# Two of the 4 MB expert loads of a mixture-of-experts layer issued as 112, 8 and 8 partitions

## The chip, the core and the metric

One core of a Trainium2 chip runs the whole program. The metric is the device time of one execution in microseconds. Two facts of the profile's notation: a DMA is issued by an engine's queue (SPq is that of SyncE), and its packets are moved by the core's 16 DMA engines.

## What is computed

One layer of a decoder trunk on 256 tokens of width 2048, in float32: four mixers side by side, an output projection, a cross attention into 256 memory tokens, and a mixture of experts. Only the last part matters here:

```python
x = x + hier_moe(rms_norm(x, ln_moe_g[l]), moe_w_group[l], moe_b_group[l],
                 moe_w_expert[l], moe_b_expert[l], moe_w_gate[l], moe_w_up[l], moe_w_down[l])

def hier_moe(...):
    ...
    g_idx = jnp.argmax(g_logits, axis=-1)                       # 1 of 4 groups
    top_val, top_idx = lax.top_k(e_logits, EXPERT_TOPK)         # 2 of its 8 experts
    ...
def expert_block(args):
    xblk, e = args
    hid = jax.nn.silu(xblk @ w_gate[e]) * (xblk @ w_up[e])
    return hid @ w_down[e]
```

There are 32 experts. Each has three weights of 4 MB (gate and up are 2048 x 512, down is 512 x 2048), 12 MB together, so that the experts' weights are 384 MB. A token uses two experts.

## The kernel before

The program is written engine by engine; all waits are explicit. The first 550 us hold the mixers, the attention and the router. Then the experts follow, every one of the 32 in order, each on a block of up to 32 tokens (`SLOTS`); experts whose tokens overflow a block get further blocks in a loop with a count read at run time.

For one block PE gathers the chosen tokens (`gather`, L1200) and turns them (`turn_rows`, L1226), multiplies them with the gate and up weights (`gate_up`, L1241, 64 matmuls), turns the result (`turn_hidden`, L1262), multiplies with the down weight (`down`, L1276, 32 matmuls) and adds the weighted rows to their tokens (`combine`, L1289, with DVE's `add`, L2573).

The weights come through five buffers of 4 MB, the "doubles", three in the tile `ring` and two in `late_ring`. One 4 MB load fills one double: partition p takes one contiguous row of 32 KB. SP issues the loads (`whole`, L512), strictly in the order gate, up, down, expert by expert. Before each it waits for the semaphore `pieces_done`, by which PE tells that the double's former weight is used up; a load is thus issued about four loads ahead of its use. On landing, a load adds 16 to the semaphore of its double, one for each of the 16 DMA engines. PE waits for that count in `gate_up` and `down`, by `arrived_main`.

The experts fall into three parts. Experts 0 to 8 use the semaphores `head_in`; the loop follows, in which expert 9 is also loaded; experts 10 to 31 use `main_in`. `main_load(n)` issues the n-th load of this last part: expert 10 + n // 3, weight n % 3. There are 66, of which the last expert's three are cut into smaller transfers, further below in the same block. `arrived_main` computes how many loads have gone to a double up to expert j, times 16:

```python
uses = len([n for n in range(3 * j) if MAIN_DOUBLES[n % 5] == d])
return main_in[d], 16 * uses
```

The tile names of the profile are these: `ring` and `late_ring` for the doubles, `x_gathered` for the turned tokens, `gate_up`, `hidden`, `y_slots` and `tokens_out` for the results of the steps above.

Of the kernel before, what the change touches and what calls it, by code (L numbers as in the profile page):

```python
# [31 lines left out]
KD = D // P  # L32
GW = 512
GC = GW // P
# [18 lines left out]
MAIN = FIRST + 1  # L53
# [123 lines left out]
LOOP_DOUBLES = [DOUBLES[(HEAD_LOADS - 3 + q) % 5] for q in range(3)]  # L177
MAIN_DOUBLES = [DOUBLES[(HEAD_LOADS + k) % 5] for k in range(5)]
MAIN_LOADS = 3 * (N_EXP - MAIN - 1)


def freed(n, first):

    return PPE * (first + n // 3) + (PPE if n % 3 == 2 else 4)


def places_of(doubles):

    g, u, d = doubles
    return [2 * g, 2 * u, 2 * g + 1, 2 * u + 1, 2 * d, 2 * d + 1]  # L190
# [38 lines left out]
def trunk(nc, inp, const_d, bucket_d, out):  # L229
    ctx = ExitStack()  # L230
    with ctx:
# [6 lines left out]
        main_in = [ctx.enter_context(nc.semaphore(f"main_in{i}")) for i in range(MOE_RING // 2)]  # L238
# [218 lines left out]
        def whole_source(e, q):  # L457

            w = inp[("moe_w_gate", "moe_w_up", "moe_w_down")[q]][0]
            return w.rearrange("e (p k) n -> p e k n", p=P)[:, e, :, :]  # L460
# [9 lines left out]
        def moe_double(d):  # L470

            w = ring if d < RING // 4 else late
            a = (d if d < RING // 4 else d - RING // 4) * 2 * WIDE
            return w[:, a:a + 2 * WIDE]
# [17 lines left out]
        def _(sp):  # L492
# [18 lines left out]
            def whole(e, q, d, arrived):  # L511
                sp.dma_start(moe_double(d).rearrange("p (k n) -> p k n", k=KD if q < 2 else GC),  # L512
                             whole_source(e, q)).then_inc(arrived[d], 16)
# [3 lines left out]
            for i, key in enumerate(PIECES):  # L517
                if i >= FRONT_RING:

                    g, q = PIECES[i - FRONT_RING]  # L520
# [66 lines left out]
            for h in range(2):  # L587
# [4 lines left out]
                for k in (4 * h, 8 + 4 * h):  # L592
                    a = FF * k
# [11 lines left out]
                whole(STREAM + n // 3, n % 3, DOUBLES[n % 5], head_in)  # L605

            def main_load(n):
                whole(MAIN + 1 + n // 3, n % 3, MAIN_DOUBLES[n % 5], main_in)

            sp.wait_ge(head["pieces_done"], freed(HEAD_LOADS - 5, STREAM))  # L610
            main_load(0)
            sp.wait_ge(s["tables"], 1)
            n_reg = sp.value_load(n_blk[0:1, 0:1], min_val=2, max_val=TABLE)
            with sp.Fori(1, n_reg) as i:
                e = sp.value_load(blk_e[0:1, bass.ds(i, 1)], min_val=0, max_val=N_EXP - 1)
                for q in range(3):
                    sp.wait_ge(head["pieces_done"], tally(i, PPE, 4 if q < 2 else PPE))
                    d = LOOP_DOUBLES[q]
                    sp.dma_start(moe_double(d).rearrange("p (e k n) -> p e k n", e=1, k=KD if q < 2 else GC),
                                 whole_source(bass.ds(e, 1), q)).then_inc(head_in[d], 16)  # L620
            main_load(1)
            for n in range(2, MAIN_LOADS - 3):
                sp.wait_ge(main["pieces_done"], freed(n - 2, 0) if n < 5 else freed(n - 5, 1))
                main_load(n)

            sp.wait_ge(main["pieces_done"], freed(MAIN_LOADS - 7, 1))
            g, u, d = (MAIN_DOUBLES[(MAIN_LOADS - 3 + q) % 5] for q in range(3))
            for q, a in ((0, g), (1, u)):
                sp.dma_start(moe_slot(2 * a).rearrange("p (k n) -> p k n", k=8),
                             whole_source(N_EXP - 1, q)[:, 0:8, :]).then_inc(main_in[a], 16)  # L630
            for q, a in ((0, g), (1, u)):
                for h in range(2):
                    k = 8 + 4 * h
                    sp.dma_start(moe_slot(2 * a + 1)[:, PIECE * h:PIECE * h + PIECE].rearrange("p (k n) -> p k n", k=4),
                                 whole_source(N_EXP - 1, q)[:, k:k + 4, :]).then_inc(s["tail_high" if h else "tail_low"], 16)
            sp.wait_ge(main["pieces_done"], freed(MAIN_LOADS - 6, 1))
            w = whole_source(N_EXP - 1, 2)
# [39 lines left out]
        def _(pe):  # L677
            task = [0]

            def fill(name, cols=512, parts=P):  # L680

                assert TASKS[task[0]] == name, (name, TASKS[task[0]])
                if task[0] >= 8:
                    pe.wait_ge(s["psum_drained"], task[0] - 7)
                task[0] += 1
                return bank[(task[0] - 1) % 8][0:parts, 0:cols]
# [99 lines left out]
            b = fill("params", cols=TAPS + NROW)  # L786
# [182 lines left out]
            b = fill("wq0")  # L969
# [209 lines left out]
            b = fill("pos0", cols=32)  # L1179
# [32 lines left out]
            b = fill("pos1", cols=32)  # L1212
# [4 lines left out]
            b = fill("cnt", cols=32)  # L1217
# [50 lines left out]
            def down(f, b, arrived_at, slots):  # L1268

                pe.wait_ge(f["hid"], tally(b, 1, 1))  # L1270
                for k in range(4):
                    if k % 2 == 0:
                        pe.wait_ge(*arrived_at(slots[k // 2]))
                    w = moe_slot(slots[k // 2])[:, PIECE * (k % 2):PIECE * (k % 2) + PIECE]
                    for c in range(COLS):
                        mm = pe.matmul(rows_bank[SLOTS * c:SLOTS * c + SLOTS, :], hidden_chunk(k),  # L1276
                                       w[:, 512 * c:512 * c + 512], start=k == 0, stop=k == 3)
                    if k % 2:
                        mm.then_inc(f["pieces_done"], 1)
# [12 lines left out]
            def last_half():  # L1292

                pe.wait_ge(main["hid"], N_EXP - MAIN)
                pe.wait_ge(*arrived_main(place[4]))
                w = moe_slot(place[4]).rearrange("p (k n) -> p k n", k=4)
                for k in range(4):
                    for c in range(COLS):
                        mm = pe.matmul(last_rows[0][SLOTS * c:SLOTS * c + SLOTS, 0:256], hidden_chunk(k),
                                       w[:, k, 256 * c:256 * c + 256], start=k == 0, stop=k == 3)  # L1300
                mm.then_inc(s["last_down"], 1)
# [136 lines left out]
            for j in range(last + 1):  # L1438
                place = places_of(LOOP_DOUBLES if j == 0 else [MAIN_DOUBLES[(3 * (j - 1) + q) % 5] for q in range(3)])

                def arrived_main(slot, j=j):
                    d = slot // 2
                    if j == 0:
                        return head_in[d], n_reg * 16 + 16 * (HEAD_LOADED[d] - 1)
                    uses = len([n for n in range(3 * j) if MAIN_DOUBLES[n % 5] == d])
                    return main_in[d], 16 * uses

                straight(main, j, last, place, arrived_main)
                if j < last:
                    down(main, j, arrived_main, place[4:6])  # L1450
# [1214 lines left out]
```

## Time and profile before

| | us |
|---|---|
| median of 3 runs | 1445.69 |
| lowest, highest | 1441.6, 1445.75 |
| the profiled execution | 1444.81 |
| its span, first to last instruction | 1442.9 |
| PE busy (matmul) | 1223.2 |
| DVE busy | 607.9 |
| ACT busy | 217.2 |

The granted TensorE clock was 0.918 of full speed over the span. Core-wide, 478.83 MB were moved by DMA, 332 GB/s over the span. Busy times of different engines overlap, and so do not add up to the span. How to read the time: the profiled execution is one run, and its span leaves out 1.9 us before the first and after the last instruction.

### The profile page before, as it was taken

The numbers are of one execution on the slowest core, as the hardware profiler recorded it, in microseconds if no ns is written. First come the engines' busy times: TensorE is split into PE (matmuls) and PEld (weight loads), VectorE is DVE, ScalarE is ACT, GpSimd is POOL, SyncE is SP. The second block draws the span as 40 slices with busy tenths as digits, with TensorE's granted clock in tenths as the row PEclk, the third lists the DMA queues.
The fourth block names the chain that finished last, engine by engine and source line by source line (L and its number), as shares of the span: only waits on it lengthen the run. The fifth ranks groups of instructions, "written<-read, shape, count | busy, mean of one in ns | idle before, by whom it ended". The sixth has DMA issues, their size and how long they took to land.

```text
span 1442.9 us, 16078 instructions
## 1 busy us (share of the span) xinstructions
PE 1223.2 (85%) x6717; PEld 580.2 (40%) x6717; DVE 607.9 (42%) x1281; ACT 217.2 (15%) x460; POOL 15.3 (1%) x31
## 2 busy tenths in 40 slices
PE   6999999999999999987677877877777778777877
PEld 5884564565885543232222222222222223222222
DVE  4889999678553452323122231223122222122122
ACT  4202011373011411101000100000000000000001
POOL 4000000000000000000000000000000000000000
PEclk9999999999999999999778988888898978889888
DMA  9433452522547579999999999999999999999997
GB/s 296 153 146 124 154 204 110 201 84 88 175 176 270 212 290 426 423 434 431 429 431 426 430 434 426 431 435 429 429 434 431 427 433 432 429 433 429 431 425 275
DMA packets 62392, 478.83 MB, mean 332 GB/s; under 512 B 13493, under 2 KB 21045, under 8 KB 44784
## 3 DMA queue, kind: packets, MB, share of 16 engines
q1 hardware_dynamic: 61056, 477.44, 80.2%
q8 instruction: 54, 0.88, 0.3%
q0 software_dynamic: 864, 0.25, 0.1%
q10 hardware_dynamic: 400, 0.10, 0.0%
q14 instruction: 18, 0.15, 0.0%
HBM read 475.67 MB, written 2.11 MB: 331 GB/s over the span
## 4 chain that ended last, share of the span: by engine, by line
PE 57%; DMA 32%; DVE 5%; ACT 4%; issue 1%; SPq 0%; DVEq 0%; ACTq 0%
DMA ring<-in_moe_w_up_dram 19%; PE bank L1241 12%; PE bank L715 10%; DMA late_ring<-in_moe_w_up_dram 8%; PE bank L1276 7%; PE bank L736 5%; PE bank L1006 5%; PE bank L1200 3%; PE bank L1262 3%; DMA late_ring<-in_moe_w_down_dram 2%; PE bank L1126 2%; DMA ring<-in_w_in_dram 2%; PE bank L1289 2%; PE bank L997 2%; PE bank L1082 1%
## 5 line engine op out<-in xcount | busy, mean ns | idle before, releaser
L1241 PE MATMUL bank<-ring,x_gathered 128*32 128x512 f32 x1216 | 263.1, 689 | 55.9 <-DMA late_ring<-in_moe_w_up_dram 32.6
L1241 PE MATMUL bank<-late_ring,x_gathered 128*32 128x512 f32 x832 | 210.8, 683 | 36.9 <-DMA ring<-in_moe_w_up_dram 35.6
L2573 DVE TENSOR_TENSOR tokens_out<-tokens_out,bank 128x512 f32<-128x512 f32 x240 | 148.6, 681 | 192.8 <-PE bank L1289 192.8
L2563 DVE SCALAR_TENSOR_TENSOR hidden<-hidden,bank 128x128 f32<-128x128 f32 x32 | 9.2, 288 | 359.6 <-ACT hidden L1794 359.6
L715 PE MATMUL bank<-ring,hT 128*128 128x512 f32 (+2 forms) x416 | 156.3, 536 | 3.4 <-ACT hT L1483 2.6
L1241 PEld LDWEIGHTS bank<-ring,x_gathered 128*32 128x32 f32 x1216 | 68.7, 124 | 151.9 <-issue 149.0
L1200 PE MATMUL bank<-x_tok,select 128*32 128x512 f32 x512 | 115.9, 1032 | 7.3 <-DVE select L2472 4.2
L715 PEld LDWEIGHTS bank<-ring,hT 128*128 128x128 f32 x416 | 78.6, 190 | 78.5 <-issue 67.0
L1276 PE MATMUL bank<-ring,hidden 128*32 128x512 f32 x560 | 90.9, 808 | 18.2 <-DVE hidden L2565 18.2
L1241 PEld LDWEIGHTS bank<-late_ring,x_gathered 128*32 128x32 f32 x832 | 55.0, 123 | 111.7 <-issue 107.3
L1289 PE MATMUL bank<-y_slots,weight_slots 32*128 32x512 f32 x496 | 72.3, 653 | 32.1 <-ACT y_slots L1799 21.7
L1262 PE MATMUL bank<-consts,gate_up 128*128 128x64 f32 x256 | 65.9, 401 | 25.0 <-ACT gate_up L1792 25.0
L736 PE MATMUL bank<-hT,ring 128*128 128x256 f32 x384 | 83.9, 380 | 2.4 <-issue 1.4
L1262 PEld LDWEIGHTS bank<-consts,gate_up 128*128 128x128 f32 x256 | 62.1, 327 | 51.8 <-issue 51.0
L736 PEld LDWEIGHTS bank<-hT,ring 128*128 128x128 f32 x384 | 72.6, 190 | 13.0 <-ACT hT L1541 1.5
L1276 PE MATMUL bank<-late_ring,hidden 128*32 128x512 f32 x416 | 64.1, 773 | 13.6 <-DVE hidden L2565 12.3
L1792 ACT ACTIVATE gate_up<-bank 128x512 f32<-128x512 f32 x32 | 19.1, 597 | 341.3 <-PE bank L1241 341.3
L2528 DVE TENSOR_TENSOR x_gathered<-bank,gain_cols 128x512 f32<-128x512 f32 x32 | 22.1, 692 | 100.8 <-PE bank L1226 100.8
L1289 PEld LDWEIGHTS bank<-y_slots,weight_slots 32*128 32x128 f32 x496 | 19.5, 183 | 110.0 <-DVE tokens_out L2573 59.4
L1276 PEld LDWEIGHTS bank<-ring,hidden 128*32 128x32 f32 x560 | 21.0, 141 | 72.8 <-issue 52.0
L2097 DVE SCALAR_TENSOR_TENSOR knT<-z_padded,param_cols,knT 128x256 f32<-128x256 f32 x120 | 47.6, 484 | 0.0
L1799 ACT ACTIVATE y_slots<-bank 128x512 f32<-128x512 f32 x31 | 18.5, 597 | 180.9 <-PE bank L1276 180.9
(438 smaller groups left out, 1182.0 us busy)
## 6 DMA issues: line engine op xcount, KB each, us to landing
ring<-in_moe_w_up_dram SPq DMA_DIRECT2D x19, 4096.0 KB, 39.2
ring<-in_moe_w_down_dram SPq DMA_DIRECT2D x16, 4096.0 KB, 29.8
ring<-in_moe_w_gate_dram SPq DMA_DIRECT2D x16, 4096.0 KB, 38.4
late_ring<-in_moe_w_down_dram SPq DMA_DIRECT2D x13, 4096.0 KB, 29.1
late_ring<-in_moe_w_gate_dram SPq DMA_DIRECT2D x12, 4096.0 KB, 39.6
late_ring<-in_moe_w_up_dram SPq DMA_DIRECT2D x10, 4096.0 KB, 39.3
ring<-in_w_in_dram SPq DMA_DIRECT2D x20, 1024.0 KB, 9.1
ring<-in_w_out_dram SPq DMA_DIRECT2D x16, 1024.0 KB, 5.7
```

The lines of the kernel that those rows point to most:

```text
L715: mm = pe.matmul(b, lhs(i)[:, P * tt:P * tt + P], piece_view(key)[:, c, at:at + cols], start=i == 0, stop=i == n - 1)
L736: mm = pe.matmul(b[:, T * f:T * f + T], piece_view(key)[:, c, a:a + P], rhs(i), start=i == 0, stop=i == n - 1)
L997: mm = pe.matmul(b, OT[:, 4 * q + c, P * tt:P * tt + P], piece_view((f"wo{n}", q))[:, c, :], start=i == (1 if tt == 0 else 0) and c == 0, ...
L1006: mm = pe.matmul(b, rows(j), weights(j), start=j == 0, stop=j == 7)
L1126: mm = pe.matmul(b, XOT[:, k, P * n:P * n + P], piece_view(("co", c))[:, k, :], start=k == 0, stop=k == XA_H - 1)
L1200: mm = pe.matmul(rows_bank[SLOTS * c:SLOTS * c + SLOTS, :], SEL[:, tt, :], X[:, tt, :].rearrange("p (f k) -> p k f", k=KD)[:, 4 * c:4 * c ...
L1241: mm = pe.matmul(gu_bank[SLOTS * c:SLOTS * c + SLOTS, :], XGT[:, at, n % 4, n // 4, :], pieces[c % 2][:, FF * (n % 8):FF * (n % 8) + FF], ...
L1262: mm = pe.matmul(turn_bank[:, 64 * k:64 * k + 64], ff, FOLD, start=True, stop=True)
L1276: mm = pe.matmul(rows_bank[SLOTS * c:SLOTS * c + SLOTS, :], hidden_chunk(k), w[:, 512 * c:512 * c + 512], start=k == 0, stop=k == 3)
L1289: mm = pe.matmul(mix[c][:, :], SWT[r, tt, :], YS[r, :], start=True, stop=True)
L2097: ins = v.scalar_tensor_tensor(acc[:, c, :], z, tap, acc[:, c, :], ALU.mult, ALU.add)
L2573: ins = v.tensor_tensor(y, x, mix[c][:, :], ALU.add)
```

## The change

Two loads of the last part, number 21 (gate weight of expert 17) and number 48 (gate weight of expert 26), are issued as three DMAs: partitions 0 to 111, 112 to 119 and 120 to 127. Each of the three adds 16 to the double's semaphore. `arrived_main` therefore counts two more for each such load. All other loads stay as they are.

```diff
+UNEVEN = (21, 48)
...
             def main_load(n):
-                whole(MAIN + 1 + n // 3, n % 3, MAIN_DOUBLES[n % 5], main_in)
+                e, q, d = MAIN + 1 + n // 3, n % 3, MAIN_DOUBLES[n % 5]
+                if n not in UNEVEN:
+                    whole(e, q, d, main_in)
+                    return
+                for a, b in ((0, 112), (112, 120), (120, 128)):
+                    sp.dma_start(moe_double(d)[a:b, :].rearrange("p (k n) -> p k n", k=KD if q < 2 else GC),
+                                 whole_source(e, q)[a:b, :, :]).then_inc(main_in[d], 16)
...
                     uses = len([n for n in range(3 * j) if MAIN_DOUBLES[n % 5] == d])
+                    uses += 2 * len([n for n in UNEVEN if n < 3 * j and MAIN_DOUBLES[n % 5] == d])
                     return main_in[d], 16 * uses
```

On SP, at load 21, the order of the instructions was this before (rows 125 to 129 of SP's instructions; a row is one DMA with its tiles, its shape and its wait):

```order
L512 DMA late_ring<-in_moe_w_up_dram 128x8192 [waits main_pieces_done]
L512 DMA ring<-in_moe_w_down_dram 128x8192 [waits main_pieces_done]
L512 DMA ring<-in_moe_w_gate_dram 128x8192 [waits main_pieces_done]
L512 DMA late_ring<-in_moe_w_up_dram 128x8192 [waits main_pieces_done]
L512 DMA ring<-in_moe_w_down_dram 128x8192 [waits main_pieces_done]
```

and it is this with the change:

```order
L513 DMA late_ring<-in_moe_w_up_dram 128x8192 [waits main_pieces_done]
L513 DMA ring<-in_moe_w_down_dram 128x8192 [waits main_pieces_done]
L614 DMA ring<-in_moe_w_gate_dram 112x8192 [waits main_pieces_done]
L614 DMA ring<-in_moe_w_gate_dram 8x8192 x2
L513 DMA late_ring<-in_moe_w_up_dram 128x8192 [waits main_pieces_done]
L513 DMA ring<-in_moe_w_down_dram 128x8192 [waits main_pieces_done]
```

One row has become two (three DMAs), with one wait as before; nothing else has changed its place. At load 48 it is the same.

## Rows read from the trace of the kernel before

**Rows 1.** The page: span, PE's busy time, DMA share in 40 slices.

```profile
span 1442.9 us, 16078 instructions
PE 1223.2 (85%) x6717; PEld 580.2 (40%) x6717; DVE 607.9 (42%) x1281; ACT 217.2 (15%) x460; POOL 15.3 (1%) x31
DMA  9433452522547579999999999999999999999997
```

**Rows 2.** DMA view of 560 to 1400 us: packets, queues.

```profile
DMA packets 12571, 361.35 MB, mean 430 GB/s; under 512 B 1399, under 2 KB 1399, under 8 KB 1399
q1 hardware_dynamic: 12531, 360.75, 100.0%
q8 instruction: 34, 0.56, 0.3%
```

**Rows 3.** Chain of 700 to 1400 us: start, length, what; DMA pieces from 912 us.

```profile
912.44 38.12 DMA ring<-in_moe_w_up_dram
...
970.54 38.33 DMA late_ring<-in_moe_w_up_dram
...
1026.04 42.59 DMA ring<-in_moe_w_up_dram
...
1086.64 40.29 DMA late_ring<-in_moe_w_up_dram
...
1144.81 40.41 DMA ring<-in_moe_w_up_dram
...
1195.46 30.13 DMA late_ring<-in_moe_w_down_dram
...
1230.98 43.15 DMA late_ring<-in_moe_w_up_dram
...
1294.61 37.82 DMA ring<-in_moe_w_up_dram
...
1352.72 37.98 DMA ring<-in_moe_w_up_dram
```

**Rows 4.** Waits of PE, 560 to 1400 us: total us, times, longest.

```profile
PE bank L1241 <- DMA ring<-in_moe_w_up_dram: 58.0, 13, 6.9
PE bank L1241 <- DMA late_ring<-in_moe_w_up_dram: 32.6, 8, 5.6
```

**Rows 5.** DMA view of 1007.0 to 1016.7 us, the time of one load.

```profile
DMA packets 144, 4.18 MB, mean 431 GB/s; under 512 B 16, under 2 KB 16, under 8 KB 16
```

**Rows 6.** Windows of 1 us at the stream's end; the last two numbers: DMA share, GB/s.

```profile
1414.00:1415.00 1.00, 0.00 (x0) 0.00 (x0) 1.00 (x2) 0.00 (x0) 0.00 (x0) 1.00 1.02 418
1425.00:1426.00 1.00, 0.40 (x4) 0.00 (x0) 0.00 (x0) 0.53 (x1) 0.00 (x0) 1.00 0.55 213
1427.00:1428.00 1.00, 1.00 (x6) 1.00 (x5) 0.00 (x0) 0.00 (x0) 0.00 (x0) 1.00 0.50 190
1428.00:1429.00 1.00, 1.00 (x4) 0.54 (x4) 0.35 (x2) 0.28 (x1) 0.00 (x0) 1.00 0.25 94
1430.00:1431.00 1.00, 1.00 (x21) 0.65 (x24) 0.00 (x0) 0.00 (x0) 0.00 (x0) 1.00 0.06 25
1431.00:1432.00 1.00, 1.00 (x28) 0.58 (x20) 0.00 (x0) 0.03 (x1) 0.00 (x0) 1.00 0.04 14
```

**Rows 7.** DMA view of 55.7 to 56.1 us, when ACT's 8-partition store runs.

```profile
DMA packets 85, 0.15 MB, mean 384 GB/s; under 512 B 8, under 2 KB 16, under 8 KB 85
q10 hardware_dynamic: 16, 0.01, 9.4%
```

**Rows 8.** Line 512, SP's loads: issue ns min/median/max; DMA to landing.

```profile
L512 SPq DMA_DIRECT2D ring<-in_moe_w_gate_dram x16: 431/432/1123, 593.9 to 1342.8; - x16
DMA to landing us min/median/max: 12.8/37.1/43.2
```

**Rows 9.** DMA view of 5.55 to 6.2 us: POOL's loads (q0) beside SP's (q1).

```profile
q1 hardware_dynamic: 31, 0.23, 84.8%
q0 software_dynamic: 24, 0.06, 24.5%
```

**Rows 10.** Chain from 1360 us, PE on the last up load; PE's longest wait after 1400 us.

```profile
1390.83 9.74 PE bank L1241 x64
...
PE bank L1289 <- DVE tokens_out L2573: 2.6, 1, 2.6
```

## The prediction

> **What bounds the kernel now.** I read the page first. Its span is 1442.9 us; the profiled execution took 1444.81 us, 0.9 us under the median of the three runs, 1445.69 us. PE is busy 85% of the span, which looks like a PE kernel, but the row of the DMA share says otherwise: 9 in every slice from the sixteenth to the last but one [rows 1]. From about 550 us on the kernel streams expert weights without a gap. The DMA view of 560 to 1400 us gives the rate, 430 GB/s, nearly all of it on q1, SP's queue; the only other traffic of note is 34 packets of q8, 0.56 MB of instructions, 16 KB each [rows 2].
>
> The chain of waits, second, shows how PE hangs on that stream. Each DMA piece there is the load of an up weight, ends when it lands, and is followed by PE's gate_up [rows 3]. The ends of those pieces (start plus length) are the clock of the stretch: 950.56, 1008.87, 1068.63, 1126.93, 1185.22, 1274.13, 1332.43, 1390.70 us. Two experts are six loads. 1332.43 - 1274.13 = 58.30 us, so a load costs 9.72 us; 1126.93 - 1068.63 is the same to a hundredth. But 1068.63 - 1008.87 = 59.76, 1.5 us more; and 1225.59, the end of a down load's piece, minus 1185.22 is 40.37 for four loads (38.87 by the rate), again 1.5 us more. So the stream is a metronome with a rare hiccup. The waits of PE say what it costs PE: 90.6 us, in 21 waits for up loads [rows 4]. A stretch on the path with waits of 4 us and more is one that the stream sets, and PE's clock or work do not: what counts is when the **slowest** DMA engine has brought its share, since PE waits for all sixteen.
>
> Are the sixteen in step? One 4 MB load is 144 packets: 128 rows of a partition, 32 KB each, and 16 small ones (under 512 B), one completion for each engine [rows 5]. So an engine brings 8 rows in 9.72 us, **1.21 us a row**. The end of the stream shows their lag, since nothing is queued behind. The DMA share is 1.02 at 1414 to 1415 us, 0.55 at 1425 and 0.50 at 1427: eight of sixteen engines have nothing left. At 1428 it is 0.25, at 1430 and 1431 0.06 and 0.04: a single engine still works [rows 6]. So eight engines are through by 1425 us or earlier, seven about 1428, one at 1432: half of them run some 5 us behind the others, and the last one 7 to 8 us behind. The hiccups fit. If 34 instruction packets fall on eight engines in turn, each gets about 4, and at 1.5 us each that is 6 us of lag, about what the end shows.
>
> **The change, part by part.** *The loads.* Main loads 21 and 48, both gate loads, go out as 112, 8 and 8 partitions. No byte is added. Counting back from the up load 61, which lands at 1390.70 us, load 48 lands near 1264 us and load 21 near 999 us (40 loads of 9.72 and two hiccups).
>
> *The shares.* 112 rows over 16 engines are 7 each. For 8 partitions the nearest row is ACT's 8-partition store of the distance table: 16 packets on q10, 8 of them completions [rows 7]. So such a transfer uses eight engines, one row each. I take both small transfers to go to the same eight. Then these bring 7 + 2 = 9 rows and the other eight 7, where each had 8. Per split, eight engines lose one row (-1.21 us) and eight gain one (+1.21 us). Over both splits that is **-2.43 us** and +2.43 us. If the lightened eight are the lagging eight, the slowest engine at the end is 2.43 us earlier, and the eight that are 7 to 8 us ahead of it stay ahead. The Trainium skill, "DMA: Bandwidth & Descriptors", section on why a DMA increments its semaphore by 16, says that the engine count is the largest up to 16 that divides the slowest dimension, and that a transfer from SP or ACT takes the lowest-numbered engines; by it both small transfers meet on engines 0 to 7, and the term stays 2.43 us.
>
> *The issue.* Two more DMA instructions per split on SP, 0.43 us each by the gate loads' row, 0.9 us. A load is issued 37.1 us before it lands (median), nearly four loads of queue, so 0.9 us hides behind them: 0. If that cover were gone it would be 1.7 us in all [rows 8]. The next SP wait, for the up load's buffer, is issued 0.9 us later at most, under the same cover.
>
> *Completions.* 32 more small packets. A load's 16 already lie inside its 9.72 us, so well under 0.1 us: 0. PE waits for 48 instead of 16 on that buffer; the gate load lands one load (9.72 us) ahead of the up load for which PE really waits, so that wait is never the last.
>
> *Place of arrival.* This is the term whose price the trace does not have: a lone transfer of 32 KB rows into 8 neighbouring partitions. From below: like any row, 1.21 us, 0 extra. The nearest row is the burst of POOL's loads at 5.55 to 6.2 us: 24 packets of q0 run beside q1's stream, which kept 84.8% of sixteen engines, and the sum did not fall under full share [rows 9]. These are short packets, but 0.06 MB written beside a full stream cost nothing that one sees. From above: rows that go to the same few partitions might queue for each other (rival 1). I take 0, by the nearer row, and keep the rest for the range.
>
> *Sum.* 1444.81 - 2.43 = 1442.4 us for a profiled execution; with the 0.9 us to the median, **1443.3 us**. When the last up load has landed at 1390.70 us, PE starts on it at 1390.83 us, and in the last 43 us it has no wait for DMA at all, the longest is 2.6 us on DVE [rows 10]; from 1390.83 us it runs its own chain of 52 us to the end of the span, so it ends earlier by what the last up load arrives earlier, if the clock's pattern is the same. That is -0.17%, and 0.3% (4.3 us) is about what a measurement of this kernel can tell from no change: so "same".
>
> **The rivals.** *1. The small transfers collide, slower.* Eight engines write 32 KB rows to 8 neighbouring partitions at once. In an ordinary load an engine's 8 rows take 9.72 us; suppose that this is also all that a group of 8 partitions can take in, and that the 8 target partitions lie in two such groups. Then four engines and the group's usual one share each, and a row takes 5 x 1.21 = 6.07 us. The loaded eight need 7 x 1.21 + 2 x 6.07 = 20.6 us instead of 9.7: +10.9 us per split, 21.8 us in all. They are 7.5 us ahead of the last one at the end, so the end moves by 21.8 - 7.5 = +14.3 us, to 1460.0 us. It decides once a split costs them over 3.75 us, against my 1.21. At half the price (10.9 us) it gives +3.4 us, 1449 us. The Trainium skill, "SBUF — State Buffer", section "Door 1: The DMA port swizzle", says just this: bandwidth follows from how many of 16 ports the partitions reach. By its table partitions 112 to 119 reach two ports and so do 120 to 127; by the rule the kernel would be at 1460 us. The burst of [rows 9] speaks mildly against it.
>
> *2. The wrong half.* If the lagging eight get the ninth row, the slowest is 2.43 us later: 1448.1 us, still within 0.3%. No view names a packet's engine. Following the packets end to end around the store of [rows 7], I find the instruction fetch of that moment on an engine that has no packet of the store; one case only, but it speaks for the lightened half.
>
> *3. It does nothing.* If the two small transfers go to different engines, the shares stay even, and the time is 1445.7 us.
>
> **How the numbers follow.** Forecast 0.55; collision 0.25 (full or at half price); wrong half 0.12; nothing 0.08. The range begins at 1440.5 us, 2.8 us under the forecast, since PE's clock moved single runs from 1441.6 to 1445.75; it reaches to 1460 us for the collision, and leaves out about 0.15. Faster by over 0.3% would need twice what is in the sum, so only scatter gives it: 0.13. Slower takes nearly all of the collision: 0.24. Same: 0.63.
>
> **What would show it.** Right: in the view of the end, the share drops to half later (1427 us for 1425) and reaches zero earlier (1429.6 us for 1432); the up loads from number 22 on land 1.2 us earlier, from number 49 on 2.4 us, and PE's 90.6 us of waits shrink by about as much once. Collision: the DMA share over the stretch around 990 and 1255 us falls well under 1 or its GB/s under 430, and the next piece of the chain is 5 us or more too long. Wrong half: pieces 1.2 us longer. Nothing: the end's shares as before.

## The result and the profile after

| | before | after |
|---|---|---|
| median of the runs, us | 1443.64 (1440.19 to 1445.75) | 1486.07 (1481.57 to 1490.44) |
| the profiled execution, us | 1444.81 | 1481.81 |
| its span, us | 1442.9 | 1480.0 |

The changed kernel is **slower**: the ratio is 1.0303, 95% interval [1.028, 1.0326], 42.4 us in the medians of four runs each and 37.0 us between the two profiled executions. The four runs of the changed kernel lie in two pairs, 1481.57 and 1481.81 us and 1490.32 and 1490.44 us; the profile is of the lower pair, and so its difference is the smaller one. I had forecast 1443.3 us, at most 1460.0.

The page of the changed kernel: span, PE, and the 40 slices of 37 us for DMA share and rate.

```profile
span 1480.0 us, 16082 instructions
...
PE 1224.8 (83%) x6717; PEld 582.0 (39%) x6717; DVE 607.7 (41%) x1281; ACT 217.0 (15%) x460; POOL 15.4 (1%) x31
...
DMA  9344352603466789999999999999999999999996
GB/s 292 145 161 140 111 199 107 248 29 116 161 239 217 299 311 427 430 429 432 430 432 430 430 432 432 428 348 340 430 431 433 428 434 429 230 413 430 432 422 235
```

PE did the same work (1224.8 us against 1223.2 in [rows 1]). The row to look at is not the share: it is 9 throughout, as before. The rate below it is not: some 430 from the sixteenth slice on, but 348 and 340 in the 27th and 28th slice (962 to 1036 us), and 230 in the 35th (1258 to 1295 us). These are the two cut loads. **Busy engines, few bytes**: a full share does not mean a full rate.

Windows of the changed kernel around load 21; the last two numbers of a row are the DMA share and GB/s. The last two rows take in each slow stretch as a whole.

```profile
975.00:980.00 5.00, 1.51 (x8) 0.46 (x12) 0.34 (x1) 0.00 (x0) 0.00 (x0) 0.60 0.99 426
985.00:990.00 5.00, 4.19 (x35) 2.14 (x27) 0.00 (x0) 0.60 (x1) 0.00 (x0) 1.00 1.00 216
1000.00:1005.00 5.00, 4.66 (x30) 1.24 (x22) 2.09 (x4) 0.98 (x2) 0.00 (x0) 1.00 1.08 210
1005.00:1010.00 5.00, 0.00 (x0) 0.00 (x0) 2.77 (x5) 0.00 (x0) 0.00 (x0) 0.68 1.01 161
1015.00:1020.00 5.00, 0.00 (x0) 0.00 (x0) 0.00 (x0) 0.00 (x0) 0.00 (x0) 0.50 1.00 433
...
983.00:1014.00 31.00, 18.67 (x122) 6.45 (x114) 7.06 (x15) 2.45 (x5) 0.00 (x0) 0.83 1.00 219
1260.00:1300.00 40.00, 21.63 (x134) 6.93 (x126) 7.06 (x15) 2.45 (x5) 0.00 (x0) 0.80 1.00 229
```

From about 983 us the 112 partitions arrive at 216 GB/s, half the 431 GB/s of [rows 5]: 1.21 us a row has become some 2.4. The single packets in the two traces say the same, and that no engine is spared: the 98 packets of 32 KB that start between 985 and 1000 us took 2.15 to 2.56 us each, where in the kernel before nearly all took 1.21 to 1.23 us. At 1005 us, about when the 8-partition transfers run, it is 161 GB/s. At 1015 us all is as before. What a slow stretch loses against the full rate is its length times (1 - rate / 431): 31 x (1 - 219 / 431) = 15.2 us, and 40 x (1 - 229 / 431) = 18.7 us. I call this figure the loss of a cut, and use it for every experiment below.

How many engines an 8-partition transfer uses can be counted from its completions, which are packets under 512 B. These are the rows of all DMA on the page of the kernel before and on that of the changed one.

```profile
DMA packets 62392, 478.83 MB, mean 332 GB/s; under 512 B 13493, under 2 KB 21045, under 8 KB 44784
...
DMA packets 62424, 478.83 MB, mean 324 GB/s; under 512 B 13525, under 2 KB 21077, under 8 KB 44816
```

There are 32 more, 16 for each cut load. A whole load has 16 completions, so a cut one has 32, which is 16 + 8 + 8; three transfers over all 16 engines would have 48. So an 8-partition transfer does take eight engines, as I read from [rows 7].

The chain of the changed kernel (start, length, what), to be laid beside [rows 3].

```profile
1004.66 18.61 another core or an unknown queue
1023.41 9.00 PE bank L1248 x64
...
1128.72 41.80 DMA late_ring<-in_moe_w_up_dram
...
1326.70 42.43 DMA ring<-in_moe_w_up_dram
...
1386.93 40.48 DMA ring<-in_moe_w_up_dram
```

PE takes the up load after load 21 at 1023.3 us (1004.66 + 18.61), where before it landed at 1008.87: **+14.4 us**. The up load that lands at 1170.52 us is three loads behind the one at 1126.93 before, so due at 1156.09: still +14.4. After load 48 the pieces end at 1369.13 and 1427.41 us, before at 1332.43 and 1390.70: **+36.7 us** both times. These two steps are the whole 37.0 us of the profiled execution: 14.4 at the first cut, 22.3 at the second. The row "another core or an unknown queue" is no other core: the table of waits below gives the same wait to the up load of `late_ring`. That load was issued at 965.00 us, so it landed 58 us after its issue, where the median before was 37.1.

PE's waits for DMA in the changed kernel, 560 to 1437 us (total us, times, longest).

```profile
PE bank L1248 <- DMA late_ring<-in_moe_w_up_dram: 73.1, 9, 21.5
PE bank L1248 <- DMA ring<-in_moe_w_up_dram: 50.6, 13, 5.8
...
PE bank L1283 <- DMA late_ring<-in_moe_w_down_dram: 5.6, 1, 5.6
```

They sum to 129.3 us. With another 1.5 us for a down load in `ring` it is 130.8 us; before, it was the 90.6 us of [rows 4] and 1.3 us for a down load, 91.9 us in all. That is +38.9 us, the same account from the other side. Loads 21 and 48 are gate loads; PE loses the time at the up load behind each, 18.7 us in one wait after load 21 and 21.5 us in one after load 48.

The end of the changed kernel's stream, windows of 1 us, as in [rows 6].

```profile
1456.00:1457.00 1.00, 1.00 (x8) 0.22 (x4) 0.00 (x0) 0.00 (x0) 0.00 (x0) 0.50 1.01 373
...
1458.00:1459.00 1.00, 1.00 (x16) 0.36 (x12) 0.00 (x0) 0.00 (x0) 0.00 (x0) 1.00 0.61 225
...
1460.00:1461.00 1.00, 1.00 (x12) 0.26 (x8) 0.00 (x0) 0.00 (x0) 0.00 (x0) 1.00 0.21 84
...
1465.00:1466.00 1.00, 1.00 (x4) 0.65 (x5) 0.28 (x1) 0.28 (x1) 0.00 (x0) 1.00 0.12 45
```

The share is full to 1457 us, 0.21 at 1460, and a share of 0.12 five us later is two engines that work alone. Before, half of the engines closed some 5 us behind the others, and one alone for the last 2 to 3 us. The two losses make 33.9 us of the 36.7. That the rest, 2.8 us, is this greater lag of the slowest is likely, but only argued; more on it under e12.

### The profile page after: what moved, and what is told of

The parts are those of the page before. It is cut to its first block, busy times and chain, and to the rows that moved or that the text cites. A ratio compares the mean times of both kernels' runs of the same rounds, so it can differ in the third digit from the quotient of the medians.

```text
span 1480.0 us, 16082 instructions
## 1 busy us (share of the span) xinstructions
PE 1224.8 (83%) x6717; PEld 582.0 (39%) x6717; DVE 607.7 (41%) x1281; ACT 217.0 (15%) x460; POOL 15.4 (1%) x31
## 4 chain that ended last, share of the span: by engine, by line
PE 56%; DMA 30%; DVE 5%; ACT 4%; another core or an unknown queue 3%; issue 1%; DVEq 0%; ACTq 0%
DMA ring<-in_moe_w_up_dram 20%; PE bank L1248 11%; PE bank L722 10%; PE bank L1283 7%; PE bank L743 6%; DMA late_ring<-in_moe_w_up_dram 5%; PE bank L1013 5%; PE bank L1207 3%; DMA late_ring<-in_moe_w_down_dram 3%; PE bank L1269 3%; DMA ring<-in_moe_w_down_dram 2%; PE bank L1133 2%; PE bank L1296 2%; PE bank L1004 2%; PE bank L706 1%
## 5 line engine op out<-in xcount | busy, mean ns | idle before, releaser
L1248 PE MATMUL bank<-late_ring,x_gathered 128*32 128x512 f32 x832 | 213.8, 690 | 41.1 <-DMA ring<-in_moe_w_up_dram 39.8
L1283 PE MATMUL bank<-ring,hidden 128*32 128x512 f32 x560 | 86.1, 770 | 18.7 <-DVE hidden L2573 17.2
L1283 PE MATMUL bank<-late_ring,hidden 128*32 128x512 f32 x416 | 68.4, 818 | 17.9 <-DVE hidden L2573 12.3
L743 PEld LDWEIGHTS bank<-hT,ring 128*128 128x128 f32 x384 | 72.6, 190 | 11.5 <-issue 1.2
L1296 PEld LDWEIGHTS bank<-y_slots,weight_slots 32*128 32x128 f32 x496 | 19.4, 183 | 110.1 <-DVE tokens_out L2581 59.4
## 6 DMA issues: line engine op xcount, KB each, us to landing
late_ring<-in_moe_w_gate_dram SPq DMA_DIRECT2D x12, 4096.0 KB, 38.9
```

The lines of the kernel that those rows point to most:

```text
L743: mm = pe.matmul(b[:, T * f:T * f + T], piece_view(key)[:, c, a:a + P], rhs(i), start=i == 0, stop=i == n - 1)
L1248: mm = pe.matmul(gu_bank[SLOTS * c:SLOTS * c + SLOTS, :], XGT[:, at, n % 4, n // 4, :], pieces[c % 2][:, FF * (n % 8):FF * (n % 8) + FF], ...
L1296: mm = pe.matmul(mix[c][:, :], SWT[r, tt, :], YS[r, :], start=True, stop=True)
```

## The experiments

Every kernel below changes only how single main loads are issued, through a table like the change's own; the semaphore count follows. "Load 12" is `main_load(12)`. Such entries are given as (first, end) or (first, end, step) of the partitions. The theories at the start: the extra transfers or their wait as such; the shape of 112 rows or its reading; uneven shares of the engines; and the place of arrival, that is, which engine writes which partitions. Of a run with several cut loads the total is compared with the sum of the losses, and each cut by its own window. The runs e1, e4, e5, e6, e8, e9 and e13 are single ones. The kernel before, measured beside them, lay between 1441 and 1450 us, so their totals are good to some 4 us at best; the rates in their windows are the better evidence.

**Five shapes (e1).**

```diff
+PARTS = {12: ((0, 64), (64, 128)), 21: ((0, 96), (96, 128)), 30: ((0, 112), (112, 128)),
+         39: tuple((16 * i, 16 * i + 16) for i in range(8)), 48: tuple((32 * i, 32 * i + 32) for i in range(4))}
```

> Five gate loads are cut in five ways, every byte moved once: load 12 as 64 + 64 partitions, 21 as 96 + 32, 30 as 112 + 16, 39 as eight times 16, 48 as four times 32. All these keep sixteen engines with equal shares. Theory P (place of arrival: a group of 8 partitions, p to p+3 and p+32 to p+35, takes rows in at the rate of one engine, 1.21 us a row; whole loads give each engine a group of its own): a cut costs by the groups that it reaches, 64 + 64 +9.7 us, 96 + 32 +4.9, 112 + 16 +4.9 or more, eight of 16 +29, four of 32 +9.7, together about +58 us. Theory S (only the odd shape of 112 rows, 7 an engine, is slow): +8.5 us at load 30 and nothing elsewhere. Theory O (each further DMA costs): by the number of DMAs, 39 most, but under 1 us each, together under 12 us.

Measured: 1525.24 us against 1444.07, +81 us for five cuts. The windows of the five slow stretches in e1:

```profile
903.00:930.00 27.00, 19.60 (x122) 6.24 (x114) 7.07 (x15) 2.45 (x5) 0.00 (x0) 0.82 1.00 225
1003.00:1032.00 29.00, 16.82 (x102) 5.72 (x94) 7.07 (x15) 2.45 (x5) 0.00 (x0) 0.84 1.00 227
1104.00:1137.00 33.00, 20.45 (x134) 6.76 (x126) 7.07 (x15) 2.45 (x5) 0.00 (x0) 0.86 1.00 224
1208.00:1242.00 34.00, 21.86 (x134) 7.06 (x126) 7.07 (x15) 2.45 (x5) 0.00 (x0) 0.80 0.99 220
1311.00:1344.00 33.00, 23.70 (x142) 7.63 (x142) 5.72 (x13) 2.45 (x5) 0.00 (x0) 0.82 1.01 253
```

Losses, in the order of the loads: 12.9, 13.7, 15.8, 16.6 and 13.6 us. They sum to 72.6 of the 81 us. All five cuts cost nearly the same, at about half the rate, whether the load is two transfers or eight. It is nothing about the number 112. The prices of theory P (4.9 us for 96 + 32, 29 for eight times 16) are as wrong as those of the other two theories.

**112 and 16, even shares (e2).**

```diff
+PARTS = {n: ((0, 112), (112, 128)) for n in (21, 48)}
```

> Loads 21 and 48 as 112 + 16 partitions: the change without its uneven shares, since 16 partitions are one row for each of sixteen engines. Theory P: the 112 part costs what it does in the change (about 17 us where 8.5 would be the full rate), the 16 rows reach 4 groups and take about 5 us instead of 1.2, together some +12 us at each place, +25 us in all, against +42 of the change. Theory U (the uneven shares, 9 rows against 7, are what costs): no more than +2 us.

Measured: 1476.72 us, ratio 1.0216 [1.014, 1.0293], +32.7 us. The two stretches in e2:

```profile
985.00:1016.00 31.00, 17.83 (x117) 6.18 (x106) 7.07 (x15) 2.45 (x5) 0.00 (x0) 0.86 1.01 211
1264.00:1299.00 35.00, 20.69 (x134) 6.83 (x126) 7.07 (x15) 2.45 (x5) 0.00 (x0) 0.79 0.99 223
```

Losses 15.8 and 16.9 us, as large as in the change. Most of the cost is there with even shares; by the medians the two small transfers in place of one account for some 5 us a cut ((42.4 - 32.7) / 2), but the interval of e2, 20 to 42 us, allows for none and for twice as much, and the losses in the windows show no difference. With uneven shares as the cause e2 would have cost 2 us at most, so they are not it.

**Cut by columns (e3).** Three transfers again, but each over all 128 partitions, with 14, 1 and 1 sixteenths of the row.

```diff
+PARTS = {n: ((0, 14), (14, 15), (15, 16)) for n in (21, 48)}
...
+                    sp.dma_start(moe_double(d)[:, FF * a:FF * b].rearrange("p (k n) -> p k n", k=b - a),
+                                 whole_source(e, q)[:, a:b, :]).then_inc(main_in[d], 16)
```

> Loads 21 and 48 as three DMAs, each over all 128 partitions, with 14, 1 and 1 of the 16 row pieces: as many DMAs, waits and bytes as in the change, but every engine writes where it writes in a whole load. Theories P and S: no change beyond 1 us. Theory O (the further DMAs, their completions or the wait for 48): about +20 us a place, as in the change.

Measured: 1444.14 us, ratio 1.0001 [0.9979, 1.0022]. At the two places, in e3:

```profile
985.00:1015.00 30.00, 25.52 (x174) 8.21 (x166) 7.07 (x15) 2.69 (x6) 0.00 (x0) 0.89 1.00 427
1255.00:1285.00 30.00, 21.84 (x154) 7.38 (x158) 8.53 (x21) 2.45 (x5) 0.00 (x0) 0.94 1.01 431
```

Per cut load two more DMAs on SP, a wait for 48, and 32 more completions: no cost within the interval of some 3 us either way. The first theory falls, and my zeros for issue and completions stand.

**Copies from memory to memory (e4).** A copy of 128, 112 and 128 rows goes ahead of loads 12, 30 and 48, into a scratch in DRAM. Nothing is left out.

```diff
+COPIES = {12: 128, 30: 112, 48: 128}
...
+                    sp.dma_start(copied_d[P * (n % 5):P * (n % 5) + rows, :].rearrange("p (k n) -> p k n", k=KD),
+                                 whole_source(MAIN + 1 + n // 3, 0)[0:rows, :, :]).then_inc(s["stored"], 16)
```

> No load is cut; ahead of loads 12, 30 and 48 a copy of expert rows from DRAM to DRAM is put in, of 128, 112 and 128 rows of 32 KB, which is added work and writes to no partition. Theory P: the copy of 112 rows costs 7/8 of one of 128 (each engine 7 rows for 8). Theory S (reading or issuing 112 rows is slow whatever the target): it costs as much as 1.75 copies of 128 rows by the row, so more than either copy of 128.

Measured: 1470.67 us, +26.6 us, in a single run. The 368 rows are 2.875 loads, 27.9 us at the usual rate; a copy of 112 rows at half rate would have added 8.5 us to that. So 112 rows that end in DRAM are read, issued and moved like any others, and the shape is free. What is slow needs SBUF as its target.

**Cuts by step (e5).**

```diff
+PARTS = {12: tuple((i, 128, 8) for i in range(8)), 30: ((0, 128, 2), (1, 128, 2)),
+         48: tuple((i, 128, 4) for i in range(4))}
```

> Load 12 as eight transfers of 16 partitions, 8 apart (the e-th of sixteen engines writes partition 8e + r, so engines 0 to 7 write partitions 0 to 63 and 8 to 15 the others, as in a whole load, but two engines meet in each group of 8 partitions); load 30 as two transfers of 64 partitions, 2 apart; load 48 as four of 32, 4 apart. Theory P (a group of 8 partitions takes one engine's rate): about +10 us at each place. Theory H (each half of the partitions takes eight engines' rate, 215 GB/s, whoever writes): load 12 +0 to +2 us; loads 30 and 48 +0 to +2 us too if an engine gets neighbouring rows of the transfer, some +13 us each if rows are dealt out in turn. Total +2 or +28 us by H, +30 us by P. Theory C (any cut by partitions costs the same 13 to 17 us): +40 us.

Measured: 1460.14 us, +15 us. At the three loads, in e5:

```profile
899.00:928.00 29.00, 18.45 (x118) 6.13 (x110) 7.07 (x15) 2.45 (x5) 0.00 (x0) 0.85 1.00 218
1085.00:1115.00 30.00, 25.84 (x158) 8.11 (x154) 7.07 (x15) 2.45 (x5) 0.00 (x0) 0.80 1.00 431
1255.00:1285.00 30.00, 21.45 (x146) 7.24 (x144) 7.79 (x17) 2.84 (x6) 0.00 (x0) 0.89 1.01 433
```

None of the three theories had this. P priced each load at 10 us, H put load 12 at 2 us at most, C expected the same 13 to 17 us for all. Two transfers of 64 partitions, free; four of 32, free; eight of 16 with step 8, loss 14.3 us. A cut into partitions is not dear in itself: 64 contiguous partitions cost 13 us (e1), every second one nothing.

**Eights, and two more shapes (e6); the eights by group (e8).**

```diff
+PARTS = {12: tuple((8 * i, 8 * i + 8) for i in range(16)), 30: ((0, 32), (32, 96), (96, 128)),
+         48: ((0, 64), (64, 128))}
```

> Load 12 as sixteen transfers of 8 neighbouring partitions, which eight engines alone move; load 30 as partitions 0 to 31, 32 to 95, 96 to 127; load 48 as 64 + 64, as in the first shapes run. Theory P: 16 times 4.9 us at load 12, +68 us. Theory H: eight engines move 16 rows each, 19.4 us, +10 us, and some more while they write the upper half against the other eight, +10 to +20 us. Load 30: +13 us by H with rows dealt in turn, +7 with neighbouring rows. Load 48: +13 us as before.

```diff
+PARTS = {12: tuple((32 * h + i, 32 * h + 32, 4) for h in range(2) for i in range(4)) + ((64, 128, 1),),
+         30: tuple((8 * i, 8 * i + 8, 1) for i in range(8)) + ((64, 128, 1),), 48: ((0, 64, 1), (64, 128, 1))}
```

> Load 12: partitions 0 to 63 by eight transfers of 8 partitions, 4 apart, so that each of the eight engines that move them writes into its own group; then partitions 64 to 127 as one. Load 30: the same with 8 neighbouring partitions each, so that four engines meet in a group. Load 48: 64 + 64. Theory P: load 30 costs 8 times 3.6 us = 29 us more than load 12. Theory H: they cost the same, within 3 us, and some 5 to 13 us each for the second half, which sixteen engines write. Load 48 as before, +13 us.

Measured: e6 1535.85 us, +90.8; e8 1539.32 us, +94.3 (both against 1445.06). First e6's three stretches, then those of e8.

```profile
895.00:950.00 55.00, 20.07 (x122) 6.37 (x114) 7.07 (x15) 2.45 (x5) 0.00 (x0) 0.66 1.01 199
1099.00:1149.00 50.00, 23.50 (x156) 8.01 (x148) 10.15 (x20) 2.91 (x7) 0.00 (x0) 0.79 0.99 236
1297.00:1358.00 61.00, 25.28 (x164) 8.25 (x156) 10.51 (x21) 3.43 (x7) 0.00 (x0) 0.74 1.00 196
```

```profile
902.00:939.00 37.00, 17.69 (x106) 5.72 (x98) 7.07 (x15) 2.45 (x5) 0.00 (x0) 0.71 1.00 205
1091.00:1148.00 57.00, 23.68 (x142) 7.61 (x142) 8.75 (x18) 2.45 (x5) 0.00 (x0) 0.71 1.00 217
1296.00:1358.00 62.00, 27.81 (x172) 8.74 (x164) 12.35 (x24) 3.44 (x7) 0.00 (x0) 0.75 1.00 195
```

Losses in e6 29.6, 22.6 and 33.3 us, in e8 19.4, 28.3 and 33.9. They sum to 85.5 of 90.8 us and 81.6 of 94.3 us. The sixteen eights cost more than any cut of e1, but far less than the 68 us of theory P and more than the 10 to 20 us of theory H; in e8 loads 30 and 12 differ by 8.9 us, where P had 29 us and H under 3. Neither theory holds. And 64 + 64, which lost 12.9 us as the first cut of e1, loses 33 to 34 as the last one here. So a cut's price seems to depend on what the kernel went through before it, and late cuts in a kernel of many are a poor measure. The next two runs have one cut each.

**One cut alone: load 21 (e7), load 48 (e12).**

```diff
+PARTS = {21: ((0, 112), (112, 120), (120, 128))}
```

> Only load 21 is cut, as 112, 8 and 8. If the two cuts of the change cost independently: half of its 42 us, +16 to +22 us. If a cut costs only through its meeting with the other: less than +8 us.

```diff
+PARTS = {48: ((0, 112), (112, 120), (120, 128))}
```

> Only load 48 is cut in 112, 8 and 8; load 21 is whole. With load 21 alone cut it was +13.5 us, with both +42.4 us. If the costs are each load's own and load 48's is simply larger (its place in the stream): +28 us here. If the second cut cost more because the first had already put the engines out of step: +13 to 16 us here, and the two single runs together fall some 14 us short of both.

Measured: e7 1458.59 us against 1445.06, ratio 1.0096 [1.0066, 1.0125], +13.5 us; e12 1461.9 us against 1443.02, ratio 1.014 [1.0118, 1.0162], +18.9 us. The stretches in e7 and in e12; the place that is left whole ran at 430 GB/s in both.

```profile
983.00:1015.00 32.00, 18.80 (x118) 6.22 (x110) 7.07 (x15) 2.45 (x5) 0.00 (x0) 0.79 0.98 200
...
1245.00:1279.00 34.00, 21.65 (x134) 7.02 (x126) 7.07 (x15) 2.45 (x5) 0.00 (x0) 0.80 1.00 211
```

The losses are 17.2 and 17.4 us. Singly the cuts cost 32.4 us in all, together 42.4. By the profiled executions (1457.43 and 1459.48 us against 1444.81) it is 12.6 and 14.7, together 27.3, against 37.0 for both. Neither expectation is met as it stands: load 21 alone fell short of the +16 to +22 us for independent cuts, and load 48 alone lies between the +13 to +16 us and the +28 us.

But the second cut of the change does not lose more at its place. The losses of the two single cuts sum to 34.6 us, those of the change to 33.9. What differs is how much of the loss reaches the end: 27.3 us of 34.6 singly, 37.0 of 33.9 together. Part of that can be seen in the last 20 us of the stream, to about its last packet, in the kernel before, the changed kernel, e7 and e12:

```profile
1413.00:1433.00 20.00, 16.97 (x138) 6.93 (x142) 5.21 (x10) 1.81 (x5) 0.00 (x0) 0.91 0.67 263
...
1448.00:1468.00 20.00, 16.02 (x114) 6.28 (x118) 5.53 (x10) 1.77 (x4) 0.00 (x0) 0.91 0.58 225
...
1427.00:1447.00 20.00, 18.16 (x154) 7.78 (x156) 4.39 (x9) 2.02 (x5) 0.00 (x0) 0.91 0.75 295
...
1427.00:1447.00 20.00, 16.58 (x134) 6.70 (x134) 5.53 (x10) 1.54 (x4) 0.00 (x0) 0.91 0.77 304
```

Engines that are through early leave the share low. It is 0.67 before, and 0.58 with both cuts: the engines end further apart. With one cut it is 0.75 and 0.77: they end closer together, and so the slowest comes later by less than the loss. Over the 20 us that is 1.8 us more idle with both cuts and 1.6 and 2.0 us less with one, or some 5 of the 10 us between the sum of the single runs and both. The lag between engines thus has a part in it. What makes one cut close the field up and a second one spread it was not tried by itself.

**Written or read? (e9).** Each of three loads goes as two transfers of 64. Load 12 writes every second partition and reads contiguous rows; load 30 does the reverse; load 48 has the step on both sides. In loads 12 and 30 rows of the weight are thereby exchanged.

```diff
+PARTS = {12: (((0, 128, 2), (0, 64, 1)), ((1, 128, 2), (64, 128, 1))),
+         30: (((0, 64, 1), (0, 128, 2)), ((64, 128, 1), (1, 128, 2))),
+         48: (((0, 128, 2), (0, 128, 2)), ((1, 128, 2), (1, 128, 2)))}
...
+                for to, of in PARTS[n]:
+                    sp.dma_start(moe_double(d)[to[0]:to[1]:to[2], :].rearrange("p (k n) -> p k n", k=KD),
+                                 whole_source(e, q)[of[0]:of[1]:of[2], :, :]).then_inc(main_in[d], 16)
```

> Which side is it, the rows that are read or the partitions that are written? Three loads go out as two transfers of 64 rows. Load 12 writes partitions with step 2 and reads contiguous halves of the rows; load 30 writes contiguous halves and reads rows with step 2; load 48 does both with step 2 (free in the run with steps). In the first two loads the rows of the weight are exchanged, so the output is another one. Place of arrival: load 12 costs 0, load 30 costs 13 us or more at about 225 GB/s, load 48 costs 0, in all +13 us. Place of reading: load 12 costs 13 us and load 30 costs 0. If only the pair counts (a given row to a given partition on a given engine), both cost, +26 us.

Measured: 1455.5 us, +12.5 us. The three places in e9:

```profile
895.00:925.00 30.00, 22.44 (x162) 7.55 (x158) 7.07 (x15) 2.45 (x5) 0.00 (x0) 0.94 1.01 432
1070.00:1101.00 31.00, 20.70 (x126) 6.66 (x118) 7.06 (x15) 2.46 (x5) 0.00 (x0) 0.83 1.00 227
1250.00:1285.00 35.00, 27.11 (x160) 8.63 (x156) 7.09 (x16) 3.43 (x7) 0.00 (x0) 0.80 1.00 428
```

432, 227 and 428 GB/s. The load that *writes* contiguous halves loses 14.7 us; the one that reads them loses nothing. **The place of arrival carries the cost**, and not the rows that are read. With e3 and e4, which clear the number of DMAs and the shape, that is the cause as far as these runs take it.

**A milder split (e10)**, a try for the 2.4 us that the change was worth in my sum.

```diff
+PARTS = {21: ((0, 128, 4), (1, 128, 4), (2, 128, 4), (3, 32, 4), (35, 64, 4), (67, 96, 4), (99, 128, 4))}
```

> Does a cut exist that lightens eight engines without the slow stretch? Load 21 alone goes out as three transfers of 32 partitions with step 4 and four of 8 partitions with step 4 (the last 32 partitions that are left). If an 8-row transfer takes the same eight engines each time, these bring 10 rows and the others 6, and only the 16 surplus rows leave the engine that has them in a whole load. If the cost follows the number of rows that change their engine: 16 of 128, some 2 us and no slow stretch at half rate; less 2.4 us if the lightened half is the lagging one, so 0 within the measurement. If any row out of place starts the slow state: a stretch of 13 to 17 us of loss as with every contiguous cut.

Measured: 1449.0 us, ratio 1.0045 [1.0026, 1.0063], +6.0 us. Its stretch:

```profile
993.00:1005.00 12.00, 11.22 (x60) 2.45 (x64) 3.41 (x8) 0.76 (x2) 0.00 (x0) 0.77 1.00 243
```

The loss is 5.2 us, a short stretch at half rate, where by the number of displaced rows some 2 us had been expected. Even 32 rows in 8-partition transfers cost more than the change could have won. No version that beats the kernel before came out of this.

**Which half lags? (e11).** Four copies of 8 rows from memory to memory ahead of load 21.

```diff
+COPIES = {21: 4}
...
+                    for i in range(COPIES[n]):
+                        sp.dma_start(copied_d[8 * i:8 * i + 8, :].rearrange("p (k n) -> p k n", k=KD),
+                                     whole_source(MAIN + 1 + n // 3, 0)[8 * i:8 * i + 8, :, :]).then_inc(s["stored"], 16)
```

> Which half lags? Ahead of load 21 go four copies of 8 rows of 32 KB from memory to memory, all landing outside the buffers; each takes eight engines with one row. Nothing is left out. As the lightened half of my forecast: the lagging engines are the other eight, the end stays where it is (+0 us, below 0.3%), and the share of busy engines at the end of the stream falls to half later (1430 us for 1425). If the lagging eight are the same ones: +4 rows of 1.21 us, +4.9 us, and the half that is ready first is ready at 1425 us as before. A copy that costs twice a row would give +9.7 us instead.

Measured: 1446.59 us against 1443.02, ratio 1.0035 [1.0018, 1.0052]. The DMA view of e11 from 960 to 992 us, where the copies are issued and land:

```profile
DMA packets 568, 13.88 MB, mean 434 GB/s; under 512 B 112, under 2 KB 112, under 8 KB 112
```

112 small packets are seven times 16: three loads and the four copies. The page of e11 bears it out: against the kernel before it has 64 more packets under 512 B and 64 more larger ones, so each of the 32 rows went in two pieces. A copy of 8 rows into DRAM is dealt over all sixteen engines, not over eight like a transfer into 8 partitions. The 32 rows then are a quarter of a load, 2.4 us for all engines alike; the measured +3.6 us (interval 2.6 to 7.5) is a little more, and the profiled execution shows no change (1444.72 against 1444.81 us). The run says nothing on which half lags; that stays open.

**By what does the loss go? (e13).**

```diff
+PARTS = {12: ((0, 128, 2), (1, 64, 2), (65, 128, 2)),
+         30: ((0, 128, 4), (1, 128, 4), (2, 128, 4), (3, 64, 4), (67, 128, 4)),
+         48: ((0, 128, 4), (1, 128, 4), (2, 128, 4), (3, 128, 8), (7, 128, 8))}
```

> By what does a cut cost: the number of rows that leave the engine that has them in a whole load, or any such row, or the small transfers as such? Three loads are cut, always with every row written to its own partition. Load 12: one transfer of 64 partitions with step 2 as in a whole load, and the other 64 as two transfers of 32 with step 2, each over half of the partitions (some 60 rows displaced). Load 30: three of 32 partitions with step 4 in place, and the last 32 as two of 16 over half of the partitions each (some 30 displaced). Load 48: the same three, and the last 32 as two of 16 partitions with step 8 (none displaced, if a transfer deals its rows to the engines in order). In the runs before, some 110 to 120 displaced rows lost 13 to 17 us, and 16 displaced rows lost 5 us. By the number of rows: about 9, 6 and 0 us. If any displaced row opens the slow state for good: 13 to 17, 13 to 17 and 0 us. If 16-partition transfers cost by themselves (the run with steps lost 14 us by eight of them): load 48 loses 3 us or more, as load 30 does or more.

Measured: 1466.02 us against 1444.7, +21.3 us. Its three stretches:

```profile
903.00:921.00 18.00, 15.03 (x78) 5.03 (x78) 4.77 (x12) 2.13 (x5) 0.00 (x0) 0.81 1.00 246
1088.00:1101.00 13.00, 11.26 (x60) 3.67 (x63) 3.45 (x10) 0.87 (x2) 0.00 (x0) 0.74 1.01 279
1268.00:1286.00 18.00, 12.63 (x82) 4.59 (x78) 6.79 (x15) 2.45 (x5) 0.00 (x0) 1.00 0.97 267
```

Losses 7.7 us for 64 rows sent out of the pattern, 4.6 and 6.9 us for 32. They sum to 19.2 of 21.3 us. That any displaced row opens a slow stretch of full length is refuted, since half the rows cost about half. The price of 0 for step 8 falls as well: load 48 lost more than load 30, as the third reading had it, by which transfers of 16 partitions cost by themselves. What holds over e1, e5, e9, e10 and e13 is 0.10 to 0.22 us for each row that goes in a transfer which is not one of the free kinds (all 128 partitions, 64 with step 2, 32 with step 4); the sixteen eights of e6 are at 0.23 us. This is a sum over what was measured, not a mechanism.

## Why the prediction was wrong

*The bound.* Right. The stream sets the time: 36.7 us later at the last up load, 37.0 us longer in all; nothing downstream took any of it back.

*The loads and the shares.* Right as far as the runs show. The two slow stretches lie where I had put loads 21 and 48, and an 8-partition transfer takes eight engines. The lag of the engines was read rightly at the end of the stream, but its source only in part: I took 1.5 us for an instruction packet, and in the trace the 34 of them took 0.99 to 1.10 us, so that four make 4 us and not 6. The 2.43 us that a lighter lagging half would give was not seen in any run; below a loss of 15 us it could not be, and e10 could not isolate it.

*Issue and completions.* Right within some 3 us: 0, by e3.

*Place of arrival.* **This is the step that failed.** I took 0 for it, "by the nearer row", the burst of POOL's loads in [rows 9]. That row is near in kind (small writes beside a full stream), but it has 24 short packets and 0.06 MB; it could not have shown a cost that grows with 32 KB rows. In its place e9 measured 14.7 us for one load of 64 + 64, at half rate, with the sides of the transfer told apart. And the term was applied to the wrong rows: I asked only what the 16 rows of the small transfers would meet, and took it for granted that the other 112 keep 1.21 us a row. They run at 216 GB/s, which is where most of the loss lies (112 rows at half rate are 8.5 of the 15.2 us).

*Rival 1.* Right in kind and side, too small in size. Its sign came as stated: GB/s under 430 at both places. It had 10.9 us a split and subtracted a lead of 7.5 us that the loaded eight had, for 14.3 us and the range's end of 1460.0. (Its half price, 1449 us, would have counted as "same", so 0.24 for slower was more than its own sum gave.) The loss was 15.2 and 18.7 us, and with both cuts nothing came off it, since all engines slow down and not the leading eight alone: every packet between 985 and 1000 us took about twice its time. That a part of the spread is used up is not wrong for one cut: in e7 and e12 the end moved by 4.6 and 2.7 us less than the loss. Its mechanism, a limit on what a group of partitions can take in, was also priced for its own two groups only. Contiguous halves show what it does over a whole load. By the Trainium skill, "SBUF — State Buffer", section "Door 1: The DMA port swizzle", partitions 0 to 63 reach eight of 16 ports, for 218 GB/s; the trace agrees (225 in e1, 227 in e9). By the same rule partitions with step 2 or step 4 reach all sixteen, and with step 8 eight: the trace agrees there too (431 and 433 against 218 GB/s in e5). But the rule leaves 0 to 95 and 0 to 111 at all sixteen ports, and so at the full rate; here they ran at half rate (227 GB/s over e1's load of 96 + 32, 216 for the 112 of the change). It also gives 16 neighbouring partitions four ports, a quarter of the rate, and e1's eight such transfers in a row ran at 220 GB/s, half of it. The measurement decides: the set of partitions is not enough. I infer that which engine writes which of them matters as well; no run shows it. The Trainium skill, "DMA: Bandwidth & Descriptors", section "Rules for kernel authors", says of two transfers to disjoint partition halves that they serialize and to use one of 128 partitions. The advice holds here; it says nothing of the 13 us by which 64 + 64 was slower than the whole load (e1).

*The wrong half, and nothing.* Neither can be judged under a loss of this size. e11 was meant for the first and does not answer it.

*Open.* Which engine writes which partition is not in any view; why 112 contiguous rows are slow and 64 with step 2 are not stays open. So does why the second cut costs 22.3 us at the place where alone it costs 14.7 (both by the profiled executions): its loss is nearly the same, 18.7 against 17.4 us, and the spread of the engines at the end accounts for a part of the rest only.

## What to carry to other kernels

Keep a large load one transfer over all 128 partitions. If it must be cut, so that a part can be used early, cut it by columns, or take every second or every fourth partition: both were free here, and contiguous ranges of partitions lost 13 to 19 us for 4 MB, in sixteen pieces of eight partitions 30 us. When pricing an unknown, ask what it does to the transfers beside it and to the large piece too, not only to the small piece that looks odd; a rival that a documented rule supports deserves more than a quarter when the only row against it is tiny.

## What was not expected

- The DMA share stays at 1.00 while the rate falls to half (216 GB/s). The row of GB/s shows what the row of shares hides.
- All engines slow down together: each 32 KB packet took 2.15 to 2.56 us in place of 1.21. Shares that are uneven between engines change the cost little: 15.8 and 16.9 us with 112 + 16, 15.2 and 18.7 us with 112 + 8 + 8.
- The number of pieces matters little down to 16 partitions: two transfers of 64 lost 12.9 us, 112 and 16 lost 15.8, eight of 16 lost 16.6. Sixteen of 8 lost 29.6.
- Cuts are not additive. The same 64 + 64 lost 12.9 us as the first cut of its kernel and 33.3 and 33.9 as the third after dearer ones. Two cuts of 112 + 8 + 8 lose no more together than singly, and still cost 10 us more in time.
- A transfer of 8 rows takes eight engines towards SBUF and all sixteen towards DRAM.
